# RWKV mixer: one schedule of rounds for heads, ends of heads and weight products, four buffer sets, joined products

## The chip, the cores and the metric

One core of a Trainium2 chip runs the whole kernel in one launch. The metric is the device time in microseconds (us) of one execution. 3 runs of the kernel before took 3470.03 to 3472.47 us, 3470.28 in the median.

## What is computed

Two transformer-like blocks, one after the other, on 256 tokens of width 2048, in float32. The first has a state-space mixer, latent attention and a convolutional feed-forward part. The second has the stage of this case: it normalises, multiplies by `w_in`, and gives parts of the product to an SSD mixer and to an RWKV-7 mixer with 32 heads of 64. The RWKV recurrence is

```
S = S * w_t + (S a_t) b_t^T + v_t k_t^T ;   y_t = S r_t
```

followed by a group norm of `y` per head, a bonus (the sum over `r * k * r_k`, times `v`) and a gate `g = sigmoid(gd) @ g2`. The change touches the order and the form of the work on RWKV, and which weight products run beside it. The result is the same function.

## The kernel before

Five instruction streams (TensorE, VectorE, ScalarE, GpSimd, SyncE) are written out by Python generators, one function of the same name in each engine's program. A `yield` ends a step; `mix` takes so many steps of each generator in turn, which makes a *round*, and `flight` runs several of a kind side by side. Since every engine's program walks the same generators in the same order, the order of the work is set there. Every engine takes its instructions in order, and semaphores (`wait_ge`, `then_inc`) hand over between engines.

**Weight products.** `linear` (L611 in TensorE's program) multiplies a weight matrix tile by tile. A *block* is 128 x 128 weights: three matmuls (L622, L623, L624: high part by high, high by low and low by high part). SyncE loads weights, ScalarE rounds the high part of a piece of up to 1024 columns (8 blocks; `cut_to`, L1889), VectorE subtracts to get the low part (L1073). In this stage a tile has 16 blocks (2 in `L_g2`) and its result is in one of two PSUM banks; VectorE scales it (`raw_shift`, L1466), ScalarE and VectorE make the token shift (L2097, L1476). `step` says how many blocks go into one step: 4 in `L_krv`, 8 in `L_sm` and `L_x`.

**A pair of heads.** `i` is a tile of 128 channels, which is two heads of 64; the code calls the work on it `pair(i)`. `krv` fills `KK(i)`, `AR(i)`, `VV(i)` for two `i` at a time (`b` is that group; below "a pair" is the two `i` of one `b`). `prep(i)` computes decay and keys (VectorE L1540 to L1581, with a reciprocal at L1568). `solve(b)` makes a triangular system in PSUM (L828), which VectorE turns (L1606, L1610) and GpSimd solves in 62 small operations (L2475, L2479); VectorE turns it back in `finish` (L1589). `block(i, hf)` works on 128 tokens, in 12 steps on TensorE: four transposes (L843 to L846), two steps of products that VectorE masks (L855, L856; L1632), `az` (L862; copied at L1636), the products with the inverse (L869, L870; its diagonal blocks are written by L1641, the result copied at L1647), `q` and the first part of the output `y0` (L876 to L882; `y0` is copied by ScalarE, L2171), `g` (L887), four chunks of 32 tokens (L897 to L901, state copied by VectorE L1663 for one half and ScalarE L2177 for the other), and a last one, where VectorE adds the chunks' outputs to `y0` (L1668). L1625 and L1627 make `bx` and `kx`, keys split by chunk. After two blocks `pair` has the tail: group norm, bonus (L911 to L919; VectorE L1684 to L1703, with a reciprocal at L1694). The next `pair` with the same parity starts only when the tail's last operation (L1703) is done.

**The order around it.** After `L_sm` and `L_krv[0]`, for b = 0 to 8, one `mix` runs `pair(2b-2)`, the weights `main(b)`, `pair(2b-1)`, and `prep` and `solve` of b. Both heads go in step. At b = 7 and 8 the weights are those of the SSD mixer (`L_bc`, `L_x`). Three buffer sets `BUF` hold k, r, v, b of three pairs. `turn_dt` (L1743) begins the next stage.

## Time and profile before

| | us |
|---|---|
| median of 3 runs | 3470.28 |
| the profiled execution, its own time | 3470.51 |
| its span, first to last instruction | 3468.4 |
| TensorE busy | 3073.7 |
| VectorE busy | 2319.8 |
| ScalarE busy | 1460.5 |
| GpSimd busy | 649.9 |

In the rows below PE is TensorE's matmul, PEld its weight load, DVE VectorE, ACT ScalarE, POOL GpSimd. `m` is an SBUF tile, `bank` a PSUM tile. Matmuls overlap in the pipeline, so TensorE's pace is read from the start of one to the start of the next. A float32 matmul appears as two instructions.

### The profile page before, as it was taken

What the parts mean: (1) busy time and instruction counts of PE and PEld (TensorE: products, weight loads), DVE (VectorE), ACT (ScalarE), POOL (GpSimd) and SP (SyncE); (2) the same over time, 40 slices, a digit from 0 to 9 for tenths busy, and PEclk for the clock granted to TensorE, in tenths of its full rate; (3) what the DMA queues carried; (4) which work ended last, traced back from release to release, by engine and by line L of the source; (5) the groups of instructions that cost most, each with busy time, mean ns of one, the idle gap of its engine ahead of it and who ended that gap; (6) DMA issues with size and microseconds to landing.
All of it is one profiled execution on the core that took longest, in us unless ns stands there. A gap on an engine that the chain in (4) does not pass through costs nothing.

```text
span 3468.4 us, 49760 instructions
## 1 busy us (share of the span) xinstructions
PE 3073.7 (89%) x19562; PEld 2716.6 (78%) x19562; DVE 2319.8 (67%) x4024; ACT 1460.5 (42%) x2307; POOL 649.9 (19%) x827
## 2 busy tenths in 40 slices
PE   5756799999999997788888888988899999999998
PEld 5645578888888887677777777986788888888887
DVE  8787467775587657677777776766575666556655
ACT  3222355554455544332333333345444444344443
POOL 5332001210021100444433334000010011001100
PEclk9877799999999998899999989999899999999999
DMA  4211145555555555212111212342355555555554
GB/s 186 89 49 49 62 150 177 188 185 176 194 193 189 167 178 176 90 63 77 68 60 65 75 68 83 119 152 76 107 170 177 178 192 183 176 200 188 189 169 147
DMA packets 78806, 475.16 MB, mean 137 GB/s; under 512 B 8112, under 2 KB 11184, under 8 KB 37424
## 3 DMA queue, kind: packets, MB, share of 16 engines
q1 hardware_dynamic: 76480, 459.66, 38.9%
q10 hardware_dynamic: 2096, 12.32, 1.0%
q8 instruction: 158, 2.59, 0.3%
q14 instruction: 72, 0.59, 0.0%
HBM read 465.66 MB, written 6.29 MB: 136 GB/s over the span
## 4 chain that ended last, share of the span: by engine, by line
PE 73%; DVE 19%; ACT 4%; issue 2%; POOL 1%; DMA 0%; DVEq 0%; SPq 0%; ACTq 0%
PE bank L620 32%; PE bank L624 20%; PE bank L622 4%; PE bank L623 4%; DVE m L1073 3%; PE bank L636 2%; ACT m L1889 1%; PE bank L899 1%; DVE m L1330 1%; DVE m L1694 1%; DVE m L1568 1%; DVE m L1723 1%; PE bank L901 1%; PE bank L900 1%; POOL m L2475 1%
## 5 line engine op out<-in xcount | busy, mean ns | idle before, releaser
L624 PE MATMUL bank<-m,m 128*128 128x256 f32 x6864 | 1951.0, 284 | 0.0
L620 PE MATMUL bank<-m,m 128*128 128x512 f32 x4992 | 1759.4, 396 | 32.0 <-DVE m L1173 13.0
L1073 DVE TENSOR_TENSOR m<-m,m 128x1024 fp32r<-128x1024 f32 (+2 forms) x944 | 1068.8, 1139 | 651.6 <-ACT m L1889 638.3
L624 PEld LDWEIGHTS bank<-m,m 128*128 128x128 f32 x6864 | 1321.8, 193 | 1.5
L1889 ACT ACTIVATE m<-m 128x1024 fp32r<-128x1024 f32 (+2 forms) x944 | 914.3, 980 | 829.1 <-PE bank L624 812.6
L620 PEld LDWEIGHTS bank<-m,m 128*128 128x128 f32 x4992 | 942.4, 189 | 248.0 <-DVE m L1173 14.9
L622 PE MATMUL bank<-m,m 128*128 128x256 f32 x1872 | 586.3, 313 | 78.4 <-DVE m L1073 45.9
L623 PE MATMUL bank<-m,m 128*128 128x256 f32 x1872 | 550.4, 294 | 0.0
L622 PEld LDWEIGHTS bank<-m,m 128*128 128x128 f32 x1872 | 380.4, 203 | 112.3 <-issue 68.5
L623 PEld LDWEIGHTS bank<-m,m 128*128 128x128 f32 x1872 | 380.7, 203 | 4.5 <-issue 3.8
L2456 POOL TENSOR_TENSOR m<-m,m 128x256 fp32r<-128x256 f32 x44 | 63.3, 1439 | 703.3 <-ACT m L2081 703.3
L2479 POOL TENSOR_TENSOR m<-m,m 128x31 f32<-128x31 f32 (+15 forms) x248 | 162.8, 657 | 19.4
L2475 POOL TENSOR_TENSOR m<-m,m 128x31 f32<-128x31 f32 (+15 forms) x248 | 153.6, 619 | 19.5
L2447 POOL TENSOR_TENSOR m<-m 128x256 f32<-128x256 f32 x44 | 32.7, 742 | 453.9 <-DVE m L1438 453.9
L2177 ACT ACTIVATE m<-bank,m 64x64 f32<-64x64 f32 x128 | 38.9, 308 | 159.3 <-PE bank L901 158.8
L636 PE MATMUL bank<-m,m 128*128 128x256 f32 x268 | 76.0, 401 | 13.0 <-ACT m L1911 12.2
L2450 POOL TENSOR_TENSOR m<-m,m 128x256 fp32r<-128x256 f32 x44 | 63.3, 1439 | 123.3 <-ACT m L2058 123.3
L2468 POOL MEMSET m<- 128x1024 f32 x8 | 7.6, 952 | 418.3 <-DVE m L1610 418.3
L2064 ACT ACTIVATE m<-bank 128x256 f32<-128x256 f32 x88 | 34.0, 386 | 116.2 <-PE bank L624 116.2
L2518 POOL TENSOR_TENSOR m<-m,m 128x256 fp32r<-128x256 f32 x8 | 6.9, 894 | 368.7 <-ACT m L2321 368.7
L2097 ACT ACTIVATE m<-m,m 128x256 f32<-128x256 f32 (+1 forms) x52 | 26.4, 507 | 116.1 <-DVE m L1466 116.0
L1443 DVE TENSOR_TENSOR m<-m,bank 128x256 f32<-128x256 f32 x88 | 37.0, 421 | 56.7 <-ACT m L2064 56.7
(361 smaller groups left out, 3268.5 us busy)
## 6 DMA issues: line engine op xcount, KB each, us to landing
m<-in_w_up SPq DMA_DIRECT2D x88, 1024.0 KB, 4.8
m<-in_w_down SPq DMA_DIRECT2D x128, 704.0 KB, 4.0
m<-in_w_gu SPq DMA_DIRECT2D x88, 1024.0 KB, 4.9
m<-in_w_out SPq DMA_DIRECT2D x48, 1024.0 KB, 5.0
m<-in_w_krv SPq DMA_DIRECT2D x48, 1024.0 KB, 4.9
m<-in_w_xbc SPq DMA_DIRECT2D x24, 1024.0 KB, 4.9
m<-in_w_z SPq DMA_DIRECT2D x16, 1024.0 KB, 4.9
m<-in_w_in SPq DMA_DIRECT2D x14, 1024.0 KB, 4.9
```

The lines of the kernel that those rows point to most:

```text
L620: pe.matmul(both, hi, x, start=kc == L.k0, stop=False)
L622: pe.matmul(ps, hi, x[:, 0, :], start=kc == L.k0, stop=False)
L623: pe.matmul(ps, hi, x[:, 1, :], start=False, stop=False)
L624: m = pe.matmul(ps, lo, x[:, 0, :], start=False, stop=last)
L636: pe.matmul(banks[N.bank][:, 0:T], ones, square_of(N, i), start=i == 0, stop=i == N.nk - 1).then_inc(*norm_pe(("sq", q)))
L1073: v.tensor_tensor(lo_of(k), raw_of(k)[0], hi_of(k).bitcast(F32), SUB).then_inc(*lo_v(("lo", k)))
L1889: a.activation(hi_of(k), src, ACT.Copy).then_inc(*hi_a(("hi", k)))
L2177: a.activation(sn[R, R], bB[R, R], ACT.Copy, scale=PL[R, i, hf * 4 + c:hf * 4 + c + 1]).then_inc(*wkv_a(("s", i, hf, c)))
L2450: g.tensor_tensor(far[:, 1, j % 22, :], s[:, 1, :], far[:, 0, j % 22, :].bitcast(F32), SUB).then_inc(*ffn_g(("lo", j)))
L2456: g.tensor_tensor(far[:, 1, j % 22, :], cvs2[j % 4], far[:, 0, j % 22, :].bitcast(F32), SUB).then_inc(*ffn_g(("lo2", j)))
L2475: g.tensor_tensor(prod, XB[:, r + 1:32, r:r + 1].broadcast_to([128, n, r + 1]), XX[:, r:r + 1, 0:r + 1].broadcast_to([128, n, r + 1]), MUL ...
L2479: g.tensor_tensor(x5, x5, prod, ADD).then_inc(*wkv_g(*([("x", b)] if r == 30 else [])))
```

## The change

`second_mixer` gives one schedule for all engines. A round has one step of an even head, two steps of weights, one of an odd head, three of weights, one of the ends of heads (`tail`), one of `prep`/`solve` (`after`). All weight products of the stage have `step=1`, one block a step. `prep` of pair b begins in round 27 + 20 b, its heads in round 56 + 20 b, odd heads five rounds later; a head takes 20 rounds, `block` has ten steps. `tail(i)` runs beside the next pair, in banks 2 and 3 and with buffers of its own. There are four buffer sets, so weights of two pairs ahead can be made. `L_g2[0]` comes after `L_krv[3]`, and so on; `L_x` is cut in 6 and 10 tiles with `L_g2[6]` and `L_g2[7]` behind them. In a block: ScalarE copies all four transposes, `az` and `wu` (VectorE did two of them); `bx` is made from the SBUF copy, `kx` is replaced by a product over 32 rows; both masks are one VectorE operation, both diagonal blocks another; the two products with the inverse are one; the chunks' outputs accumulate in PSUM on `y0`; what a head's first chunk multiplies by the zero state is left out.

```diff
+def timed(*items):
+    n = 0
+    for begin, g in items:
+        while n < begin:
+            n += 1
+            yield
+        for _ in g:
+            n += 1
+            yield
+AFTER, PAIRS, ROUNDS = 27, 56, 20
+def second_mixer(main, block, tail, after, *early):
+    def heads(e):
+        return timed(*((PAIRS + ROUNDS * b + 5 * e, chain(block(2 * b + e, 0), block(2 * b + e, 1))) for b in range(8)))
+    tails = timed(*((PAIRS + ROUNDS * (i // 2 + 1) + 5 * (i % 2), tail(i)) for i in range(16)))
+    afters = timed(*((AFTER + ROUNDS * b, after(b)) for b in range(8)))
+    run(mix((heads(0), 1), (main, 2), (heads(1), 1), (main, 3), (tails, 1), (afters, 1), *((g, 1) for g in early)))
...
-        BUF = [(alloc(2, 2, 2, 128), alloc(2, T), alloc(2, T), alloc(2, T)) for _ in range(3)]
+        BUF = [(alloc(2, 2, 2, 128), alloc(2, T), alloc(2, T), alloc(2, T)) for _ in range(4)]
...
+            return BUF[(i // 2 + 2) % 4][0][:, i % 2]
...
-        L_sm = linear("w_sm", 4, 16, TWO, lambda t: wkv_v["raw", t])
-        L_krv = [linear("w_krv", 6, 16, TWO, lambda t: wkv_v["raw", 4 + t], step=4)]
...
+        L_sm = linear("w_sm", 4, 16, TWO, lambda t: wkv_v["raw", t], step=1)
+        L_krv, L_g2, L_x = [], [], []
+        def g2(b):
+            L_g2.append(linear("w_g2", 2, 2, TWO, lambda t: wkv_v["gate", t], t0=2 * b, step=1))
+        for b_ in range(8):
+            if b_ >= 4:
+                g2(b_ - 4)
+            L_krv.append(linear("w_krv", 6, 16, TWO, lambda t: wkv_v["raw", 4 + t], t0=6 * b_, step=1))
+        g2(4)
+        L_bc = linear("w_xbc", 8, 16, TWO, lambda t: ssd_v["raw", t], t0=16, step=1)
+        g2(5)
+        for t0, nt in ((0, 6), (6, 10)):
+            L_x.append(linear("w_xbc", nt, 16, TWO, lambda t: ssd_v["raw", t], t0=t0, step=1))
+            g2(6 + len(L_x) - 1)
...
-                if hf:
-                    pe.wait_ge(*wkv_v["y2", i, 0])
-                elif i >= 2:
-                    pe.wait_ge(*wkv_v["out", i - 2])
+                if before:
+                    pe.wait_ge(*wkv_a["y", *before])
...
-                for e in range(2):
-                    R, b = HALVES[e], (bB, bA)[e]
-                    if e:
-                        pe.wait_ge(*wkv_v["kx", i, hf])
-                    elif hf:
-                        pe.wait_ge(*wkv_v["s", i, 0, 3])
-                        pe.wait_ge(*wkv_a["s", i, 0, 3])
+                pe.wait_ge(*wkv_a["tk", i, hf])
+                if before:
+                    pe.wait_ge(*wkv_v["s", *before, 3])
+                    pe.wait_ge(*wkv_a["s", *before, 3])
+                for e, R, b in ((0, HALVES[0], bA), (1, HALVES[1], bB)):
                     pe.matmul(b[:, 0:128], BB(i)[R, TS], AR(i)[R, hf, 1, :], start=True, stop=True)
+                for e, R, b in ((0, HALVES[0], bA), (1, HALVES[1], bB)):
                     pe.matmul(b[:, 128:384], KK(i)[R, TS], AR(i)[R, hf, :, :].rearrange("p a b -> p (a b)"),
                               start=True, stop=True).then_inc(*wkv_pe(("mk", i, hf, e)))
-                    yield
-                pe.wait_ge(*wkv_a["tk", i, hf])
-                pe.wait_ge(*wkv_v["mk", i, hf, 1])
+                yield
+                pe.wait_ge(*wkv_v["mk", i, hf])
...
-                    xb = xbd[2 * e_ + e]
-                    pe.matmul(bA[:, 64 * e:64 * e + 64], xb, tk[:, 0, 64 * e:64 * e + 64], start=True, stop=True)
-                    m = pe.matmul(bA[:, 128 + 64 * e:192 + 64 * e], xb, az[e_][:, 64 * e:64 * e + 64], start=True,
-                                  stop=True)
+                    m = pe.matmul(bA[:, 0:256].rearrange("p (a b) -> p a b", a=2)[:, :, 64 * e:64 * e + 64],
+                                  xbd[e_][:, e, :], tk[:, TZ:TV, 64 * e:64 * e + 64], start=True, stop=True)
...
                 pe.wait_ge(*wkv_v["g", i, hf])
                 for c in range(4):
+                    Q, first = slice(32 * c, 32 * c + 32), hf == c == 0
+                    sb_ = sbd[2 * e_ + c % 2]
                     if c:
                         pe.wait_ge(*wkv_v["s", i, hf, c - 1])
                         pe.wait_ge(*wkv_a["s", i, hf, c - 1])
-                    sb_ = sbd[2 * e_ + c % 2]
-                    pe.matmul(bA[:, 32 * c:32 * c + 32], sb_, qb[:, 32 * c:32 * c + 32], start=True,
-                              stop=True).then_inc(*wkv_pe(("yc", i, hf, c)))
-                    pe.matmul(bB[:, 0:128], bxb[:, c, :], wub[:, 128:256], start=True, stop=False)
-                    pe.matmul(bB[:, 0:128], kxb[:, c, :], tk[:, 1, :], start=False, stop=False)
-                    pe.matmul(bB[:, 0:128], gb[:, c, :], sb_, start=False, stop=True).then_inc(
-                        *wkv_pe(("s", i, hf, c)))
-                    yield
-                yield
+                    if not first:
+                        m = pe.matmul(bA[:, Q], sb_, qb[:, Q], start=False, stop=c == 3)
+                        if c == 3:
+                            m.then_inc(*wkv_pe(("y", i, hf)))
+                    pe.matmul(bB[:, 0:128], bxb[:, c, :], wub[:, 0:128], start=True, stop=False)
+                    m = pe.matmul(bB[:, 0:128], tk[Q, TK, :], tk[Q, TV, :], start=False, stop=first)
+                    if not first:
+                        m = pe.matmul(bB[:, 0:128], gb[:, c, :], sb_, start=False, stop=True)
+                    m.then_inc(*wkv_pe(("s", i, hf, c)))
+                    yield
...
+            def tail(i):
                 e = i % 2
+                b, b2 = banks[2 + e], banks[3 - e]
+                pe.wait_ge(*wkv_a["y", i, 1])
+                if i:
+                    pe.wait_ge(*wkv_v["out", i - 1])
+                for k in range(2):
+                    pe.wait_ge(*wkv_v["xa", min(i // 2 + 2, 7), k])
+                pe.matmul(b[:, 0:T], blk, ybs[e], start=True, stop=True).then_inc(*wkv_pe(("t1", i)))
                 yield
                 pe.wait_ge(*wkv_a["t2", i])
+                pe.matmul(b2[:, 0:T], blk, tails[1], start=True, stop=True).then_inc(*wkv_pe(("t2", i)))
                 pe.wait_ge(*wkv_v["t3", i])
+                pe.matmul(b[:, 0:T], blk, ybs[e], start=True, stop=True).then_inc(*wkv_pe(("t3", i)))
+                yield
...
-                v.tensor_tensor(bxb, bA[:, 256:384].unsqueeze(1).broadcast_to([128, 4, 128]), m4, MUL).then_inc(
-                    *wkv_v())
-                v.tensor_tensor(kxb, bA[:, 384:512].unsqueeze(1).broadcast_to([128, 4, 128]), m4, MUL).then_inc(
-                    *wkv_v(("kx", i, hf)))
+                else:
+                    v.wait_ge(*wkv_g["zero"])
                 yield
                 for e in range(2):
                     v.wait_ge(*wkv_pe["mk", i, hf, e])
-                    v.tensor_tensor(mk[e].rearrange("p a b -> p (a b)"), (bB, bA)[e][:, 0:384], m3, MUL).then_inc(
-                        *wkv_v(("mk", i, hf, e)))
-                    yield
-                v.wait_ge(*wkv_pe["az", i, hf])
-                v.tensor_copy(az[e_], bB[:, 0:128]).then_inc(*wkv_v())
+                v.tensor_tensor(mk.rearrange("p e a b -> p e (a b)"),
+                                pair_.rearrange("p (e x) -> p e x", e=2)[:, :, 0:384],
+                                m3.unsqueeze(1).broadcast_to([128, 2, 384]), MUL).then_inc(*wkv_v(("mk", i, hf)))
+                yield
                 finish(i // 2)
                 v.wait_ge(*wkv_v["xt", i // 2])
-                for e in range(2):
-                    ln = hf * 4 + i % 2 * 2 + e
-                    v.tensor_tensor(xbd[2 * e_ + e].rearrange("p (c t) -> p c t", c=4),
-                                    XTs[i // 2 % 2][:, :, ln].unsqueeze(1).broadcast_to([128, 4, 32]),
-                                    bm.rearrange("p (c t) -> p c t", c=4), MUL).then_inc(
-                        *wkv_v(*([("xb", i, hf)] if e else [])))
-                yield
-                v.wait_ge(*wkv_pe["wu", i, hf])
-                v.tensor_copy(wub, bA[:, 0:256]).then_inc(*wkv_v(("wu", i, hf)))
+                ln = hf * 4 + i % 2 * 2
+                v.tensor_tensor(xbd[e_].rearrange("p e (c t) -> p e c t", c=4),
+                                XTs[i // 2 % 2][:, :, ln:ln + 2].rearrange("p t e -> p e t").unsqueeze(2).broadcast_to(
+                                    [128, 2, 4, 32]),
+                                bm.rearrange("p (c t) -> p c t", c=4).unsqueeze(1).broadcast_to([128, 2, 4, 32]),
+                                MUL).then_inc(*wkv_v(("xb", i, hf)))
+                yield
+                v.wait_ge(*wkv_a["tk", i, hf])
+                v.tensor_tensor(bxb, tk[:, TB, :].unsqueeze(1).broadcast_to([128, 4, 128]), m4, MUL).then_inc(
+                    *wkv_v(("bx", i, hf)))
                 yield
...
-                v.tensor_tensor(ybuf[:, TS], ybuf[:, TS], bA[:, 0:128], ADD).then_inc(*wkv_v(("y2", i, hf)))
...
-                a.activation(tokb[e_].rearrange("p a b -> p (a b)"), bA[:, 0:256], ACT.Copy).then_inc(
-                    *wkv_a(("tk", i, hf)))
-                for _ in range(5):
-                    yield
-                a.wait_ge(*wkv_pe["y0", i, hf])
-                if hf == 0 and i >= 2:
-                    a.wait_ge(*wkv_v["out", i - 2])
-                a.activation(ybs[e_][:, TS], bA[:, 0:128], ACT.Copy).then_inc(*wkv_a(("y0", i, hf)))
+                if hf or i >= 2:
+                    a.wait_ge(*wkv_pe["s", *((i, 0) if hf else (i - 2, 1)), 3])
+                a.activation(tk[:, TA:, :].rearrange("p a b -> p (a b)"), bA, ACT.Copy).then_inc(*wkv_a(("tk", i, hf)))
+                yield
+                yield
+                a.wait_ge(*wkv_pe["az", i, hf])
+                a.activation(tk[:, TZ, :], bB[:, 0:128], ACT.Copy).then_inc(*wkv_a(("az", i, hf)))
+                yield
+                a.wait_ge(*wkv_pe["wu", i, hf])
+                a.activation(wu[e_], bA[:, 0:256], ACT.Copy).then_inc(*wkv_a(("wu", i, hf)))
+                yield
                 yield
                 yield
                 for c in range(4):
                     R, sn = HALVES[1], sbd[2 * e_ + (c + 1) % 2]
+                    if c == 3:
+                        a.wait_ge(*wkv_pe["y", i, hf])
+                        if i >= 2:
+                            a.wait_ge(*wkv_v["out", i - 2])
+                        a.activation(ybs[e_][:, TS], bA[:, 0:128], ACT.Copy).then_inc(*wkv_a(("y", i, hf)))
...
```

## Rows read from the trace of the kernel before

**Rows 1.** The page: busy time and share of the span by engine.

```profile
PE 3073.7 (89%) x19562; PEld 2716.6 (78%) x19562; DVE 2319.8 (67%) x4024; ACT 1460.5 (42%) x2307; POOL 649.9 (19%) x827
```

**Rows 2.** Windows of the stage: us, busy (instructions) of five engines, clock, DMA, GB/s.

```profile
1310.00:1357.00 47.00, 30.63 (x221) 29.67 (x221) 39.05 (x69) 18.17 (x25) 4.32 (x9) 0.82 0.24 81
1357.00:1387.00 30.00, 29.30 (x250) 29.13 (x249) 17.53 (x23) 14.20 (x18) 0.00 (x0) 1.00 0.93 329
1387.00:1434.40 47.40, 38.05 (x307) 36.99 (x306) 35.47 (x61) 21.82 (x31) 15.43 (x21) 0.93 0.35 116
1434.40:1533.50 99.10, 78.71 (x574) 70.36 (x573) 62.97 (x128) 29.37 (x56) 64.61 (x104) 0.86 0.19 65
1672.00:1770.50 98.50, 83.47 (x623) 74.85 (x621) 71.55 (x151) 33.02 (x62) 40.54 (x64) 0.93 0.20 70
```

**Rows 3.** The line at which the next stage begins: ns, first and last start.

```profile
L1743 DVE COPY m<-bank x1: 224/224/224, 2317.1 to 2317.1; 128x64 f32<-128x64 f32 x1
```

**Rows 4.** TensorE's waits in one period, 1672 to 1770.5: us, times, longest.

```profile
PE bank L843 <- DVE m L1703: 5.6, 1, 5.6
PE bank L869 <- DVE m L1641: 2.7, 2, 2.3
PE bank L828 <- DVE m L1581: 2.1, 1, 2.1
...
PE bank L897 <- DVE m L1663: 1.2, 1, 1.2
```

**Rows 5.** Timeline of TensorE, full clock: start us, us, what, instructions in a row.

```profile
1623.10 0.39 PE L900 MATMUL bank<-m,m 128*128 128x128 f32 x2
...
1623.32 0.39 PE L901 MATMUL bank<-m,m 128*128 128x128 f32 x2
...
1712.38 0.39 PE L870 MATMUL bank<-m,m 128*128 128x64 f32 x2
1712.60 0.39 PE L869 MATMUL bank<-m,m 128*128 128x64 f32 x2
...
1714.00 0.38 PE L622 MATMUL bank<-m,m 128*128 128x256 f32 x1
1714.22 0.28 PE L623 MATMUL bank<-m,m 128*128 128x256 f32 x1
1714.34 0.28 PE L624 MATMUL bank<-m,m 128*128 128x256 f32 x1
```

**Rows 6.** VectorE's groups in that period: busy us, mean ns, idle before them.

```profile
L1073 DVE TENSOR_TENSOR m<-m,m 128x1024 fp32r<-128x1024 f32 (+1 forms) x13 | 15.9, 1221 | 4.9 <-ACT m L1889 4.9
L1632 DVE TENSOR_TENSOR m<-bank,m 128x384 f32<-128x384 f32 x8 | 4.3, 548 | 0.8 <-PE bank L856 0.8
...
L1476 DVE SCALAR_TENSOR_TENSOR m<-m,m,m 128x256 f32<-128x256 f32 x6 | 3.6, 608 | 3.5 <-ACT m L2097 3.5
L1568 DVE RECIPROCAL m<-m 128x256 f32<-128x256 f32 x2 | 3.5, 1753 | 0.1
...
L1641 DVE TENSOR_TENSOR m<-m,m 128x128 f32<-128x128 f32 x8 | 3.3, 447 | 0.0
L1627 DVE TENSOR_TENSOR m<-bank,m 128x512 f32<-128x512 f32 x4 | 2.7, 678 | 0.0
...
L1647 DVE COPY m<-bank 128x256 f32<-128x256 f32 x4 | 1.7, 422 | 3.0 <-PE bank L870 3.0
...
L1636 DVE COPY m<-bank 128x128 f32<-128x128 f32 x4 | 1.1, 280 | 0.0
...
L1668 DVE TENSOR_TENSOR m<-m,bank 128x128 f32<-128x128 f32 x4 | 0.9, 270 | 0.0
```

**Rows 7.** L1641 with `solve` running, then without; GpSimd's L2479 from the page.

```profile
L1641 DVE TENSOR_TENSOR m<-m,m x4: 369/485/717, 1609.3 to 1611.0; 128x128 f32<-128x128 f32 x4
...
L1641 DVE TENSOR_TENSOR m<-m,m x4: 373/379/381, 1664.8 to 1665.9; 128x128 f32<-128x128 f32 x4
...
L2479 POOL TENSOR_TENSOR m<-m,m 128x31 f32<-128x31 f32 (+15 forms) x248 | 162.8, 657 | 19.4
```

More of the change, by code:

```diff
@@ L942, in turn_dt, with after @@
+            def after(b):
+                yield from flight(lambda i: prep(2 * b + i), 2, 2)
+                yield from solve(b)
             def turn_dt():
@@ L1029, in tensor_program @@
                            *(L_up[q].freed(44 * q + t) for t in range(40, 44)), done=sums_ if q else None))
[L1030 to L1039 removed]
+            second_mixer(main(), block, tail, after, iter(range(8)), last_squares(sums_))
             turn_dt()
@@ L1493, in steps_dt @@
                 a, e, w, p = (q[R, :] for q in scr[0:4])
-                yield
+                for _ in range(5):
+                    yield
                 v.wait_ge(*wkv_v["dt"])
@@ L1840, in vector_program @@
             v.wait_ge(*wkv_v.last)
-            run(mix((chain(linear(L_sm, small), linear(L_krv[0], krv)), 1), (steps_dt(), 1),
-                    (both_rates(ffn_v.last), 1)))
-            v.wait_ge(*wkv_g["zero"])
-            for b in range(9):
-                before = [pair(2 * b - 2 + i) if b > 0 else iter(()) for i in range(2)]
-                after = chain(flight(lambda i: prep(2 * b + i), 2, 2), solve(b)) if b < 8 else iter(())
-                run(mix((before[0], 1), (main(b), 1), (before[1], 1), (after, 1)))
-            run(linear(L_g2[7], gated))
-            v.wait_ge(st_y[7 % 3], 16 * (7 // 3 + 1))
+            second_mixer(main(), block, tail, after, steps_dt(), both_rates(ffn_v.last))
+            for b in (5, 6, 7):
+                v.wait_ge(st_y[b % 3], 16 * (b // 3 + 1))
             turn_dt()
@@ L2116, in steps_dt @@
                 R = slice(96, 128)
-                yield
+                for _ in range(5):
+                    yield
                 a.wait_ge(*dt_v["w"])
@@ L2153, in prep @@
                 yield
-                yield
             def solve(b):
@@ L2179, in block, with tail @@
                     yield
-                yield
-            def pair(i):
-                s1, s2 = tails[2 * (i % 2)], tails[2 * (i % 2) + 1]
-                for hf in range(2):
-                    yield from block(i, hf)
+            def tail(i):
+                s1, s2 = tails
                 a.wait_ge(*wkv_v["t1", i])
@@ L2301, in both_rates @@
                 a.dma_start(a2s[0:96, :], d["a2"]).then_inc(ld_a2, 16)
-            run(mix((chain(linear(L_sm, small), linear(L_krv[0], krv)), 1), (steps_dt(), 1), (both_rates(), 1)))
-            a.wait_ge(*wkv_g["zero"])
-            for b in range(9):
-                before = [pair(2 * b - 2 + i) if b > 0 else iter(()) for i in range(2)]
-                after = chain(flight(lambda i: prep(2 * b + i), 2, 2), solve(b)) if b < 8 else iter(())
-                run(mix((before[0], 1), (main(b), 1), (before[1], 1), (after, 1)))
-            run(linear(L_g2[7], lambda t: None))
-            store(7)
+            second_mixer(main(), block, tail, after, steps_dt(), both_rates())
             for b in (5, 6, 7):
@@ L2506, in pool_program @@
                 run(linear(L_down[q]))
-            run(linear(L_sm, small))
-            g.wait_ge(*norm_v["lo", N_two.x0 + 15])
-            for q in (XA, *gt, *sbd):
-                g.memset(q, 0.0).then_inc(*wkv_g(*([("zero",)] if q is sbd[-1] else [])))
-            for b in range(9):
-                before = [pair() if b > 0 else iter(()) for i in range(2)]
-                after = chain(flight(lambda i: iter(range(5)), 2, 2), solve(b)) if b < 8 else iter(())
-                run(mix((before[0], 1), (main(b), 1), (before[1], 1), (after, 1)))
+            second_mixer(main(), block, tail, after)
             g.wait_ge(ld_y, 16)
```

249 lines of the change are left out of this document (126 added, 123 removed).

## The prediction

> **What bounds the kernel now.** I read the page first for the span and the shares: TensorE is busy 89% of it and VectorE 67% [rows 1], so TensorE is the engine to watch, but a mean over the span says nothing of the stage that is changed. So next the windows, cut at the stage's own marks [rows 2]: from 1310 us, where the first `L_sm` matmuls start, to 2317.1, where `turn_dt` copies [rows 3], is 1007 us. It has three parts: 77 us with weights alone, 47 us with the first `prep`, and then periods of 98.5 to 99 us, each of which does 100 blocks of weights and one pair (two tiles `i`). In such a period (1672 to 1770.5) TensorE is busy 83.5 us of 98.5, VectorE 71.6, ScalarE 33.0 [rows 2]. So 15.0 us per period are idle on TensorE, and its granted clock is 0.93: about 14% of the time at 1.2 and the rest at 2.4 GHz. The work in those 14% (13.8 us) would take half as long at the full clock, so the clock costs up to 6.9 us, and the period's work at 2.4 GHz is 83.5 - 6.9 = 76.6 us. No engine is the bound: 22 us of each 98.5 are waits and what they cost in clock. The waits of TensorE say which [rows 4]: 5.6 us for the last operation of a head's tail (L1703 to L843), 2.7 for the diagonal blocks of the inverse (L1641), 2.1 for `prep` (L1581), the rest smaller.
>
> **What a change can get at most.** The stage has 1248 blocks (64 of `L_sm`, 768 of `L_krv`, 32 of `L_g2`, 384 of `w_xbc`). A block is three matmuls of 0.12 us start to start at the full clock (1714.22 to 1714.34 [rows 5]), 0.36 us, so 449 us. A pair's own work is 76.6 - 36 = 40.6, eight of them 325. Together 774, against 1007: 233 us are there to be had.
>
> **The change, step by step.** One round now has five blocks of weights, and a pair has 20 rounds. I count the 250 rounds (1248 / 5) in four stretches.
>
> Rounds 0 to 27 (135 blocks). Before, the first 80 blocks took 47 us (to 1357), with VectorE busy 39 of them and the clock at 0.82; the next 83 took 30 [rows 2]. The rates and the `steps_dt` chain are the same instructions, four rounds later, with less to do per round but five blocks instead of eight to hide them. I take the same 47, and 55 blocks at 0.36: 67 us.
>
> Rounds 27 to 56 (145 blocks, two `prep` and `solve`, no heads). The window with one of each and 96 blocks took 47.4 [rows 2], 13 over its weights. A round's cover is five blocks instead of four, so I take 10 over the weights for each: 145 x 0.36 + 20 = 72 us.
>
> Rounds 56 to 216 (eight pairs, 800 blocks), x us each, less 7 for the two pairs with no `prep` beside them (38.05 busy less 34.6 of weights [rows 2] is 3.5 for one). Now x.
> - TensorE. The joined `wu` product halves its instructions: 8 of the 16 pairs of L869 and L870 go. A pair is 0.22 us start to start with 64 columns, and with 128 too (L900 to L901) [rows 5], so -1.8. More turns between weights and heads, each 0.1 over the usual step (1714.00 to 1714.22 against 1714.22 to 1714.34 [rows 5]), perhaps ten more: +1. The K = 32 product instead of `kx` streams the same columns: 0. Two products less in a head's first chunk: under 0.1. 76.6 - 1.8 + 1 = 75.8.
> - VectorE. `kx` (2.7), the copies of `az` (1.1) and `wu` (1.7), the sum of the outputs (0.9) and a memset (0.3, too small to list) go [rows 6]. Two masks in one: 384 columns take 0.548, and L1627 shows 512 in 0.678, 1.02 ns per column, so 768 take 0.94 instead of 1.10: -0.6 for four. The diagonal blocks in one: between 0.57 (the slope again) and 0.88 (no gain) instead of 0.88, I take 0.7: -0.7. `bx` now reads SBUF instead of PSUM: L1641, which reads SBUF twice, took 373 to 381 ns with GpSimd quiet and up to 717 with `solve` running [rows 7]; so 0 to 0.34 more, four times, +0.6 at the middle. Sum -7.4, so 64.2 busy. Waits inside its line that stay: 4.9 for the high part of a cut and 3.5 for the shift's first half [rows 6]. 73 us of work and fixed waits per period, under TensorE's 76.
> - On that port: the Trainium skill, SBUF — State Buffer (the section on what causes contention), says that a VectorE operation with two SBUF inputs and a GpSimd operation that reads SBUF take one shared port pair as an exclusive lock, and the loser waits. By that rule a whole GpSimd operation, 0.66 us on the mean (L2479 [rows 7]), could stand before each `bx`: 2.6 us instead of 0.6, VectorE at 75, still under TensorE, and the sum the same. The trace agrees in kind.
> - ScalarE takes the two copies (0.28 and 0.42 each on VectorE, L1636 and L1647 [rows 6]; I take the same) and a `tk` of twice the width (256 columns more, 0.3): 4 x 1.0, so 37 of some 85 busy. Cover: 48 us idle. Its copies stand in line behind a 1 us cut, so the price is a late copy at worst.
> - The stall of 5.6 us at the next head's first transposes goes: they wait now for the copy of the previous output (`y`), and the tail has four rounds of its own; the next to wait for it is `gate`, four rounds later. What is late next: VectorE in `prep`. A `prep` and `solve` of a pair is 35.5 - 96 x 0.21 = 15.3 us of VectorE (0.21 a block by the window before it [rows 2]), now in eight rounds: 1.9 each, on the 2.4 of the rest (49 / 20), 4.3 against TensorE's 3.8, and two of them hold two reciprocals of 1.75 each [rows 6]. Eight such rounds leave it 4 us or more behind, and its slack is less than a round: 3 us idle. Every other handoff (mask to `az`, `q` to `g`, `g` to chunk, sums to the next chunk) has at least two or three blocks and the other head's step between: 0 if VectorE is on time, up to the old 9.4 (15.0 - 5.6) if not; I take 3.5. So 6.5 idle.
> - Clock: 6.9 went with 15 idle; with 6.5, 2.7 by proportion. Bounds 0 and 6.9.
> x = 75.8 + 6.5 + 2.7 = 85. Eight times, less 7: 673 us.
>
> Rounds 216 to 250 (168 blocks, last tail, two gates, the wait for the last store): 60.5 + 4.5 = 65 us.
>
> Priced at nothing: the fourth buffer set and the index shift (no work moves); the loads' order on SyncE (same bytes, at 70 GB/s [rows 2]); GpSimd's memsets placed inside the stream (it idles for them); ScalarE's wait for the saved `h` (eight rounds, 14 us, lie between; if not landed it holds cuts for a few us, once).
>
> Sum: 67 + 72 + 673 + 65 = 877, against 1007: -130. The profiled execution took 3470.5 us with a span of 3468.4, the median of the runs is 3470.3, so the execution and the median are the same for this purpose. 3470 - 130 = **3340 us**. A change within 0.2% (7 us) is what a measurement here can't tell from none.
>
> **Rivals.**
> 1. The waits stay, elsewhere. VectorE (73) and TensorE (76) are so near each other that two lines kept in step by in-order waits lose as much as before. For it: VectorE already shows 27 us of waits per period, and the row of cuts among them. Against: its load falls by 8. x = 95: 130 - 80 = 50 gained, 3420. The Trainium skill has a rule that ends in the same place (TensorE: Matmul & The Clock Gate, section on the second HAM failure mode: short idles between groups of matmuls in every iteration let the clock go back and forth). As rows: at 0.86, as in 1434 to 1533 [rows 2], 75.8 us of work take 88, and with 6.5 idle x is again 95. Against it, the period with 15 us idle still has 0.93 [rows 2].
> 2. TensorE nearly fed: 1 us idle, no clock lost, x = 78: 56 more, 3284.
> 3. Slower: each of 20 rounds ends on one handoff that isn't covered. The place is the sum of a chunk: VectorE's copy of it for the even head stands behind the cut, the shift and the tail operations of the round before, and the next chunk's matmul waits. It decides from x = 101.3, that is 16.3 us or 0.8 per round over my x. A cut (1.22) ahead of the copy in every round would do it: 20 x 1.22 = 24 us, x = 109, 3532. Against: now TensorE waits 1.2 us in a period for these copies (L897 behind L1663 [rows 4]), and only 13 cuts come in 20 rounds [rows 6].
> 4. It doesn't do what it says: the period is held by a chain that the change keeps (GpSimd's `solve`, 40.5 busy of 98.5 [rows 2]). The diagonal blocks now wait for it 24 rounds after its start, so there is no such hold. It gives 3470.
>
> **Chances.** Forecast (3300 to 3385) 0.58; first rival 0.22; second 0.14; third 0.03; fourth 0.03. The range reaches from the second rival's end to the first's: 3285 to 3420. Faster 0.94, same 0.02, slower 0.04.
>
> **What the profile after would show.** Period between the first reciprocals of `prep` near 85 us instead of 98.5; TensorE's idle time before the first transposes gone; VectorE busy near 64 per period; ScalarE near 37; clock over 0.95 between the pairs; the last tail some 30 rounds before the stage's end. I am wrong if TensorE's waits for VectorE's sums or masks sum to over 10 us per period, if the clock falls below 0.9, or if the stretch before the first head grows past 150 us.

## The result, and the profile after

The changed kernel takes 3479.24 us (median of 11 runs, 3477.6 to 3481.77), the kernel before 3471.84 beside it (11 runs): ratio 1.0022, 95% interval 1.0013 to 1.0031. It is slower by 7 us, little but clear of the interval, where 130 us less were forecast. The profiled execution took 3480.06 us.

The stage ends where `turn_dt` copies, as in [rows 3]:

```profile
L1771 DVE COPY m<-bank x1: 225/225/225, 2328.0 to 2328.0; 128x64 f32<-128x64 f32 x1
```

Counted from the same mark, 1310 us, the stage takes 1018 us where it took 1007. The mark is round: the last product of the stage ahead of it starts at 1300.5 us before, at 1303.3 in the changed kernel, 1303.8 in e7 and 1300.6 in e9 (runs below), so 3 us of a first stretch can be its arrival. The page's busy line, beside [rows 1]:

```profile
PE 3109.5 (89%) x19370; PEld 2725.0 (78%) x19370; DVE 2276.2 (65%) x3816; ACT 1496.4 (43%) x2375; POOL 666.1 (19%) x827
```

VectorE has the 44 us less work, ScalarE the 36 us more. TensorE has 192 matmuls less and is busy 36 us longer. Windows of the stage (columns as in [rows 2]): up to the first head's transposes in two parts, two periods, the stretch after the last pair has begun, the whole stage:

```profile
1310.00:1393.00 83.00, 60.34 (x449) 58.78 (x448) 52.64 (x87) 31.24 (x42) 3.87 (x9) 0.85 0.47 159
1393.00:1483.70 90.70, 63.27 (x439) 60.62 (x440) 64.31 (x103) 35.10 (x52) 46.23 (x64) 0.83 0.27 93
1667.40:1762.50 95.10, 88.39 (x598) 76.23 (x597) 65.70 (x125) 36.89 (x70) 42.75 (x65) 0.89 0.21 73
1762.50:1855.30 92.80, 84.73 (x598) 72.87 (x597) 65.75 (x125) 36.89 (x70) 42.24 (x65) 0.94 0.22 75
2139.10:2328.00 188.90, 163.23 (x1134) 146.91 (x1133) 110.98 (x190) 76.61 (x122) 0.00 (x0) 0.89 0.29 100
1310.00:2328.00 1018.00, 885.00 (x6117) 782.35 (x6117) 670.25 (x1203) 398.85 (x692) 345.98 (x521) 0.90 0.25 87
```

The kernel before over its whole stage:

```profile
1310.00:2317.10 1007.10, 842.87 (x6294) 767.98 (x6294) 714.39 (x1410) 363.01 (x624) 329.59 (x521) 0.92 0.25 87
```

TensorE's idle time did fall, from 164 us to 133; its busy time rose by 42, in fewer matmuls at a lower clock. VectorE's waits in the whole stage, of the kernel before and then of the changed one (us, times, longest):

```profile
DVE m L1073 <- ACT m L1889: 78.6, 79, 2.7
DVE m L1663 <- PE bank L901: 40.9, 37, 3.5
```

```profile
DVE m L1107 <- ACT m L1911: 154.2, 129, 3.6
DVE m L1510 <- ACT m L2119: 31.7, 52, 0.9
```

L1107 (L1073 before) is VectorE's half of a cut, the low part; it needs the high part that ScalarE makes (L1911, L1889 before). That wait has doubled, and it is the largest in the stage. TensorE's own list is short and mixed (25.1 us of the first row and 15.6 of the second lie ahead of the first head):

```profile
PE bank L652 <- DVE m L1500: 40.8, 9, 17.2
PE bank L861 <- DVE m L1616: 25.9, 8, 8.0
PE bank L899 <- DVE m L1670: 10.9, 9, 3.3
PE bank L849 <- ACT m L2166: 10.9, 6, 2.9
```

How the wait comes about stands in the timelines of TensorE, ScalarE and VectorE (start us, us, what, and in brackets the idle time before):

```profile
1688.94 0.27 PE L878 MATMUL bank<-m,m 128*128 128x128 f32 x1
...
1689.26 0.60 ACT L2189 ACTIVATE m<-bank 128x512 f32<-128x512 f32 x1 [2.77 <-PE bank L878]
1689.88 1.06 ACT L1911 ACTIVATE m<-m 128x1024 fp32r<-128x1024 f32 x1
...
1690.97 1.23 DVE L1107 TENSOR_TENSOR m<-m,m 128x1024 fp32r<-128x1024 f32 x1 [1.98 <-ACT m L1911]
1692.23 0.42 DVE L1703 SCALAR_TENSOR_TENSOR m<-bank,m 128x256 f32<-128x256 f32 x1
1692.69 0.49 DVE L1706 SCALAR_TENSOR_TENSOR m<-m,m,m 128x256 f32<-128x256 f32 x1
1693.09 0.27 DVE L1694 TENSOR_SCALAR m<-bank,m 64x64 f32<-64x64 f32 x1
1693.29 0.94 DVE L1663 TENSOR_TENSOR m<-bank,m 128x768 f32<-128x768 f32 x1
```

ScalarE's cut waits for nothing itself. It stands behind the copy of four transposes (L2189), for which ScalarE has waited 2.77 us. (This copy is of two transposes in the kernel before; `az` and `wu` are the two that are new on ScalarE.) VectorE reaches its own half of the same piece in the same step, so it waits for ScalarE's queue, and behind it stand the tail's first operations, a chunk's sums (L1694) and a mask (L1663).

By stretches (a table put together from the start times of a pair's first transposes; us; "later" is VectorE's half of a cut one piece later, the runs below):

```
                                  to 1st head   7 periods   rest    stage
before                                  124.5       725.0   157.6  1007.1
predicted                               139         591.5   146.5   877
after                                   173.7       655.4   188.8  1018.0
e1  masked keys back                    172.0       641.4   181.1   994.5
e9  later                               157.6       613.8   165.1   936.5
e7  masked keys back, later             161.0       596.8   162.7   920.5
e10 the same, later in all linears      152.5       596.8   162.7   912.0
```

### The profile page after: what moved, and what is told of

Its sections match the earlier page's. It is cut to its first block, busy times and chain, and to the rows that moved or that the text cites. A ratio compares the mean times of both kernels' runs of the same rounds, so it can differ in the third digit from the quotient of the medians.

```text
span 3478.0 us, 49231 instructions
## 1 busy us (share of the span) xinstructions
PE 3109.5 (89%) x19370; PEld 2725.0 (78%) x19370; DVE 2276.2 (65%) x3816; ACT 1496.4 (43%) x2375; POOL 666.1 (19%) x827
## 4 chain that ended last, share of the span: by engine, by line
PE 75%; DVE 17%; ACT 5%; issue 2%; DMA 1%; DVEq 0%; ACTq 0%; POOL 0%; SPq 0%
PE bank L650 32%; PE bank L654 20%; PE bank L652 5%; PE bank L653 4%; DVE m L1107 3%; ACT m L1911 2%; PE bank L666 2%; PE bank L931 1%; DVE m L1744 1%; PE bank L933 1%; DVE m L1364 1%; PE bank L930 1%; DVE m L1603 1%; PE bank L916 1%; PE bank L899 1%
## 5 line engine op out<-in xcount | busy, mean ns | idle before, releaser
L654 PE MATMUL bank<-m,m 128*128 128x256 f32 x6864 | 1958.4, 285 | 0.0
L1107 DVE TENSOR_TENSOR m<-m,m 128x1024 fp32r<-128x1024 f32 (+1 forms) x944 | 1071.3, 1142 | 730.6 <-ACT m L1911 717.0
L1911 ACT ACTIVATE m<-m 128x1024 fp32r<-128x1024 f32 (+1 forms) x944 | 913.8, 979 | 826.1 <-PE bank L654 806.1
L652 PE MATMUL bank<-m,m 128*128 128x256 f32 x1872 | 610.0, 326 | 104.7 <-DVE m L1107 44.8
L653 PE MATMUL bank<-m,m 128*128 128x256 f32 x1872 | 555.8, 297 | 0.0
L2512 POOL TENSOR_TENSOR m<-m,m 128x31 f32<-128x31 f32 (+15 forms) x248 | 175.5, 707 | 19.4
L2508 POOL TENSOR_TENSOR m<-m,m 128x31 f32<-128x31 f32 (+15 forms) x248 | 157.8, 636 | 19.5
L666 PE MATMUL bank<-m,m 128*128 128x256 f32 x268 | 77.2, 407 | 13.0 <-ACT m L1933 12.2
```

What stands on the lines that cost most here:

```text
L652: pe.matmul(ps, hi, x[:, 0, :], start=kc == L.k0, stop=False)
L653: pe.matmul(ps, hi, x[:, 1, :], start=False, stop=False)
L654: m = pe.matmul(ps, lo, x[:, 0, :], start=False, stop=last)
L666: pe.matmul(banks[N.bank][:, 0:T], ones, square_of(N, i), start=i == 0, stop=i == N.nk - 1).then_inc(*norm_pe(("sq", q)))
L1107: v.tensor_tensor(lo_of(k), raw_of(k)[0], hi_of(k).bitcast(F32), SUB).then_inc(*lo_v(("lo", k)))
L1911: a.activation(hi_of(k), src, ACT.Copy).then_inc(*hi_a(("hi", k)))
```

## The experiments

The runs are called by the first part of their names, e1 for `e1_kx`. All times are medians beside the kernel before, which gave 3471 to 3473 us each time.

**The two terms suspected first.** The changed kernel with the masked keys of before, and the kernel before without them:

```diff
-m = pe.matmul(bB[:, 0:128], tk[Q, TK, :], tk[Q, TV, :], start=False, stop=first)
+m = pe.matmul(bB[:, 0:128], kxb[:, c, :], tk[:, TV, :], start=False, stop=first)
```

> The changed kernel with one thing undone: the product of a chunk that takes 32 token rows out of 128 is again a product of all 128 rows with a masked copy of the keys (two masked copies of 128x512 a head on VectorE in place of one). Theory 1, the 32-row product costs TensorE a change of its row window: a chunk goes back from 1.19 us to 0.89 us from first product to next linear piece; 16 chunks a period of two heads, so 4.8 us a period less TensorE time, eight periods: 38 us, so about 3441 us for 3479. Theory 2, VectorE bounds the period (65.7 us busy and waits for cuts): TensorE's gain turns into waits and VectorE's extra 2 x 1.3 us or so a period lengthen it: 3479 to 3500 us.

> The kernel before with one thing done: the masked copy of the keys goes, and the chunk's key-value product takes 32 of the 128 token rows. Theory 1 (the 32-row product costs 0.3 us a chunk on TensorE): 128 chunks, of which the period's TensorE is the bound, so +38 us at most, less what the 1.3 us copy per head gives back where its wait was on the path: 3490 to 3510 us for 3471. Theory 2 (the product costs nothing by itself, the changed kernel loses in its schedule): 3471 or up to 15 us less.

e1 took 3459.28 us, 20 less than the changed kernel, and e2 3515.88, 44 more than the kernel before. So the 32-row product, which I had priced at nothing, costs; e2 is 6 us past theory 1's range. A chunk in the changed kernel, then in e1:

```profile
1703.12 0.30 PE L927 MATMUL bank<-m,m 128*128 128x32 f32 x2
1703.26 0.47 PE L930 MATMUL bank<-m,m 128*128 128x128 f32 x2
1703.65 0.48 PE L931 MATMUL bank<-m 32*128 32x128 f32 x2
1704.07 0.49 PE L933 MATMUL bank<-m,m 128*128 128x128 f32 x2
1704.31 0.37 PE L652 MATMUL bank<-m,m 128*128 128x256 f32 x1
```

```profile
1691.61 0.30 PE L927 MATMUL bank<-m,m 128*128 128x32 f32 x2
1691.75 0.47 PE L930 MATMUL bank<-m,m 128*128 128x128 f32 x2
1692.05 0.39 PE L931 MATMUL bank<-m,m 128*128 128x128 f32 x2
1692.28 0.39 PE L933 MATMUL bank<-m,m 128*128 128x128 f32 x2
1692.42 0.37 PE L652 MATMUL bank<-m,m 128*128 128x256 f32 x1
```

From L927 to the next weights it is 1.19 us with the 32-row product and 0.81 without, 0.38 a chunk. The chunks with four products and the full clock have the same medians in the two traces (95 of them in the changed kernel, 99 in e1). 128 chunks are 49 us. In the kernel before the price shows nearly in full, though the edit also takes a masked copy off VectorE and widens one on ScalarE. In the changed one less than half of it comes back:

```profile
1659.60:1751.90 92.30, 79.56 (x598) 70.72 (x597) 67.99 (x129) 36.92 (x70) 43.70 (x64) 0.93 0.22 75
```

TensorE is busy 5 to 9 us less in e1's period, and idle 12.7 us instead of 6.7 and 8.1. Something else holds the period. Theory 1 had the mechanism and twice its worth; theory 2 is against the sign, but its thought that VectorE holds the period was not refuted.

**The start as before.** Its edit, in short: `L_sm` in steps of eight and `L_krv[0]` in steps of four run ahead of the rounds, and `AFTER, PAIRS` are 0 and 29.

> The changed kernel with the start of the mixer as before: the small linear in steps of eight and the first key-receptance-value block in steps of four run beside the rate work before the rounds begin, and the rounds carry blocks 1 to 7. Theory 1 (the start's one-by-one steps lose the time, 55.5 us for the first 80 pieces where VectorE normalises 16 tiles in the way): the first head's transposes come 15 to 20 us earlier than 1483.7 us, the rest as it was, about 3462 us. Theory 2 (the start only moves a wait that the rounds after it take back): within 5 us of 3479.

3523.15 us, 44 slower; the first transposes came 3 us earlier, not 15 (the "pieces" of the expectation are blocks of 128 rows). Both theories fall. The experiment changed more than it meant to: the linears now stand five rounds otherwise against the heads, and with that the period from 1674.7 us is 102.2 us long. Why this phase is so bad stays open.

**Both halves of the cut later.** For VectorE and for ScalarE:

```diff
 if what == "piece":
-    cut_to(at_ + CUT)
+    cut_to(at_ + CUT - (1 if L.step == 1 else 0))
```

> The changed kernel with VectorE and ScalarE cutting each evacuated piece one step later in their order (a piece of lead less), linears in steps of one only. Theory 1 (VectorE and TensorE go in lockstep: VectorE waits 12.7 us a period for cuts that it asks for a piece too early): these waits fall to about 4 us, the period by 2 to 5 us, total 15 to 35 us less: about 3455 us. Theory 2 (the waits are slack of an engine that does not bound): no change, 3474 to 3484 us.

3470.26 us, 9 less, between the two theories. Its waits for cuts in the period from 1658.4 us did not fall, against theory 1:

```profile
DVE m L1107 <- ACT m L1911: 12.8, 11, 3.9
DVE m L1510 <- ACT m L2119: 3.9, 6, 0.9
```

With both halves moved VectorE still asks in the step in which ScalarE makes its half. So the ring of four buffers, which TensorE must free, isn't what VectorE waits for. The two edits together:

> The masked keys of the run e1_kx (3459.3 us) together with the later cuts of e4_lead (3470.3 us for 3479.2 of the changed kernel). Theory 1, the two costs are separate (TensorE's row window in the period, and the pieces' ring in the stretches before and after the heads): they add, 3450 us. Theory 2, both come out of the same wait (VectorE's handoffs): no more than one of them counts, 3458 to 3460 us.

3458.77 us: theory 2's number; the 9 us did not add.

**VectorE's half alone one piece later.** The same line in VectorE's program only, ScalarE as it was:

> The masked keys of e1_kx, and the later cut on VectorE alone: ScalarE still cuts at once, VectorE one piece later, so that VectorE finds its half ready. Theory 1 (VectorE's 12.7 us a period of waits for ScalarE's half of the cut delay its handoffs to TensorE): these waits fall below 4 us a period, TensorE's waits for masks and sums (some 9 us a period in e1_kx) fall by 2 to 4 us, total 3425 to 3445 us. Theory 2 (VectorE has that slack anyway): 3455 to 3462 us, as e1_kx.

3382.27 us (ratio to before 0.9743, 0.9728 to 0.9758), 77 less than e1, more than theory 1 gave. On the changed kernel without another edit, and on the kernel before (there for steps of four):

> The changed kernel with the one edit that brought e7_kx_vlead from 3459.3 to 3382.3 us: VectorE makes its half of a piece's cut one piece later than ScalarE. Theory 1 (the chain piece read by TensorE, ScalarE's half, VectorE's half, which VectorE waits for in front of everything else it has to do, is what the one-by-one steps brought; it costs the whole 77 us by itself): 3479 less 60 to 80 us, 3400 to 3420 us, and beside e7 the 32-row product then costs 20 to 40 us. Theory 2 (with the 32-row product TensorE's own work bounds the period, so that half the gain is covered): 3430 to 3450 us.

> The kernel before with VectorE's half of a cut one piece later in the linears with steps of four. Theory 1 (the wait came with the change, by its one-by-one steps; before, VectorE waits 4.9 us a period for ScalarE's half): 0 to 25 us less than 3471. Theory 2 (the wait costs both kernels the same, and the change lost elsewhere): 60 to 80 us less, 3390 to 3410 us.

e9 took 3398.18 us, 81 less than the changed kernel; e11 3447.39, 25 less than the kernel before beside it. Both are theory 1's numbers (e9 2 us past its range), but beside e7 the 32-row product costs 16 us and not the 20 to 40 expected. The later request is worth more than three times as much in the changed kernel, where it also takes more wait away: 154.2 to 4.1 us in the stage, for 78.6 to 29.7 in e11, which leaves the linears with other steps as they were.

The comparison that leaves least beside the wait is e9 with e4. VectorE's program is the same in both, with the same order of cuts, masks and sums. Only ScalarE's half stands a piece later in e4, and e4 takes 72 us more. So the gain isn't that VectorE's own cut of 1.2 us gave way to other work; it is that ScalarE's half is ready when VectorE asks for it. e9's whole stage, one of its periods, its last stretch, and the two largest waits of VectorE in the stage:

```profile
1310.00:2246.50 936.50, 842.59 (x6124) 745.44 (x6123) 668.58 (x1202) 399.13 (x692) 357.71 (x521) 0.95 0.28 95
...
1640.20:1729.00 88.80, 82.41 (x599) 70.96 (x598) 65.49 (x125) 36.93 (x70) 44.57 (x64) 0.96 0.23 78
...
2081.40:2246.50 165.10, 153.18 (x1152) 138.88 (x1150) 110.40 (x190) 76.70 (x122) 0.00 (x0) 0.98 0.35 117
```

```profile
DVE m L1694 <- PE bank L933: 49.9, 37, 3.5
DVE m L1500 <- PE bank L654: 44.7, 24, 3.8
```

The work is the same: as many matmuls but for a few that a trace misses, and on VectorE and ScalarE the same busy time within 2 us. VectorE's waits are now for TensorE: it is ahead of it, where it was behind. TensorE is idle 94 us instead of 133, which is 39 of the 81.5, and busy 42 less in the same matmuls at a clock of 0.95 instead of 0.90. In a middle period nearly all of it is the second: 95.1 us with 6.7 idle became 88.8 with 6.4. These are the stretches of the two periods by granted clock, first the changed kernel's, then e9's:

```profile
1667.40:1724.50 57.10, 54.03 (x396) 46.76 (x394) 37.71 (x69) 21.82 (x44) 41.00 (x62) 1.00 0.23 79
1724.50:1731.30 6.80, 5.98 (x27) 4.82 (x28) 4.39 (x11) 4.96 (x10) 0.00 (x0) 0.50 0.00 0
1731.30:1745.00 13.70, 12.38 (x86) 10.13 (x84) 9.24 (x16) 6.04 (x10) 0.00 (x0) 1.00 0.29 97
1745.00:1758.70 13.70, 12.19 (x59) 11.26 (x60) 11.20 (x27) 2.44 (x6) 0.00 (x0) 0.50 0.22 78
```

```profile
1640.20:1698.00 57.80, 54.24 (x396) 46.88 (x394) 38.95 (x69) 21.52 (x42) 44.57 (x64) 1.00 0.24 78
1698.00:1704.80 6.80, 5.41 (x24) 4.25 (x25) 5.05 (x13) 5.29 (x10) 0.00 (x0) 0.50 0.32 96
1704.80:1729.00 24.20, 22.77 (x180) 19.84 (x180) 21.49 (x44) 10.12 (x18) 0.00 (x0) 1.00 0.20 72
```

Both have 6.8 us at the lower of the clock's two levels (0.50, which is 1.2 GHz). The changed kernel has 13.7 us more of it from 1745.0 on, after TensorE had waited 0.3 us and 0.8 us for VectorE's and ScalarE's results; e9 has neither these waits nor the fall; its one wait from 1704.8 on, 1.4 us for `prep`, brought none. Over the seven periods the clock stood at the lower level for 116 us in the changed kernel and for 55 in e9.

The same place in a head in e9, VectorE's timeline:

```profile
1661.98 0.88 DVE L1687 TENSOR_TENSOR m<-bank,m 64x256 f32<-64x256 f32 x2 [0.88 <-PE bank L916]
1662.88 1.22 DVE L1107 TENSOR_TENSOR m<-m,m 128x1024 fp32r<-128x1024 f32 x1
1664.63 0.42 DVE L1703 SCALAR_TENSOR_TENSOR m<-bank,m 128x256 f32<-128x256 f32 x1 [0.52 <-PE bank L945]
...
1667.12 0.96 DVE L1663 TENSOR_TENSOR m<-bank,m 128x768 f32<-128x768 f32 x1 [1.27 <-PE bank L887]
```

The mask (L1663), which had stood in a row behind the late cut, is now waited for by VectorE until TensorE's product is there.

**What made the wait longer.** The changed kernel with the copies of `az` and `wu` on VectorE again (L2193 and L2196 off ScalarE):

> The changed kernel with the copies of the products az and wu on VectorE again, as before, and off ScalarE; nothing else. It tells why VectorE waits 12.7 us a period for ScalarE's half of a cut, 4.9 before. Theory 1 (the cut stands in ScalarE's line behind the two copies, which wait for TensorE): the waits fall to 5 to 8 us a period; VectorE takes 2.8 us more work, so that the period gains 1 to 5 us, 3440 to 3475 us. Theory 2 (the waits come from where the one-by-one steps put the cut among the steps of heads, whatever ScalarE carries): the waits stay over 11 us, and the period grows by the copies, 3485 to 3510 us.

3488.67 us, 9 more. VectorE's waits for cuts in the period that starts at 1670.4 us fell from 12.7 to 7.6, as theory 1 says; the time is theory 2's, 3485 to 3510, and not theory 1's, since VectorE's own work grew:

```profile
DVE m L1107 <- ACT m L1915: 7.6, 7, 2.0
```

So with the copies moved back 5 of the 8 us go that the wait grew by; over the seven periods it is 38.2 us in the kernel before, 90.9 in the changed one and 60.7 in e18. Part of the 30 can be that VectorE, with more work, asks later; this isn't separated. The moved copies are worth 9 us where they are, and it was their company with the cut that cost. The rest has other items in it: where the waits of the seven periods are followed back in the trace, about 22 of the 90.9 us stand behind the copies of `az` and `wu`, 10 behind that of the transposes, and 18 behind two small operations of `prep` and of the tail (L2175, L2218), for which ScalarE itself waits for VectorE.

**In all linears.** `- 1` for every linear of VectorE's program: with the masked keys, for the kernel before, and for the changed kernel alone:

> e7_kx_vlead with VectorE's later cut in every linear of the kernel, not only in those with steps of one. Theory 1 (the wait hurts only where VectorE has other work that TensorE waits for, in the two mixers): within 8 us of 3382. Theory 2 (it costs wherever pieces are cut): 20 us less or more.

> The kernel before with VectorE's half of each cut one piece later in every linear. It is the other side of e10_kx_vlead_all (3363 us) and e16_vlead_all. Theory 1 (the wait outside the mixer's rounds costs both kernels the same 19 us, which e10 gained over e7): 3447 less 15 to 23 us, 3424 to 3432 us, and the change proper, with the cut's wait gone from both, is worth 50 us. Theory 2 (the 19 us of e10 came from its own schedule): 3440 to 3448 us.

> The changed kernel with VectorE's half one piece later in every linear, and nothing else. Theory 1 (the 32-row product costs what e9_vlead less e7_kx_vlead showed, 16 us): 3363 plus 12 to 20 us, 3375 to 3383 us. Theory 2 (with all cuts out of the way TensorE's work is bare, and the product costs its whole 4.8 us a period): 3395 to 3402 us.

They took 3363.21, 3442.04 and 3383.93 us; e16 is 1 us past theory 1's range. Theory 1 of e10 (no gain elsewhere) falls: of the 24 us between the two profiled spans (3383.5 and 3359.3), 8.5 lie ahead of the first head and the rest outside the stage (4.5 of the 8.5 are there on arrival: the stage before ends at 1303.8 us in e7 and 1299.3 in e10). e13 gains only 5 over e11, where theory 1 wanted 15 to 23: outside the stage it has 12 less (3440.5 less 992.8 against 3443.7 less 983.5), and 9 of them are given back within it. Set e16 against e13 and the change is worth 58 us, ratio 0.983, once neither kernel has this wait. e16 against e10 prices the product at 21 us.

**The odd heads' offset.** `5 * e` taken out of `heads`, in the changed kernel and in e7:

> The changed kernel with one thing undone: the odd head of a pair in the same rounds as the even one instead of five rounds behind; the ends of heads stay where they are. Theory 1 (the offset spreads heavy rounds so that the waits of the two heads don't fall together): without it both heads' products for masks, sums and turns meet in the same rounds, and the period grows by 3 to 8 us, total 25 to 65 us more, 3505 to 3545 us. Theory 2 (each round is bound by TensorE's own work, wherever a head's steps lie): within 8 us of 3479.

> e7_kx_vlead with the odd head in the rounds of the even one instead of five behind. Theory 1 (the offset spreads the load, and the cuts' chain hid that in e6_instep, which took 3478.6 us for 3479.2): now it costs, 3395 to 3430 us. Theory 2 (the rounds are bound by work, wherever a step lies): 3378 to 3387 us.

3478.61 us for 3479.24: nothing. With the wait gone 3389.75 for 3382.27: the offset is worth 7 us, between the two theories. The changed kernel paid for it and didn't get it.

**Linear steps spread in the round.** In e8 (beside e5) and e15 (beside e10) the last of a round's five linear steps moves behind the step of the ends of heads; in e17 the five stand as two, one, one and one:

> e5_kx_lead with the last of a round's five linear steps moved behind the step of the heads' ends, so that the products of heads stand in three places between linear steps and not two. Theory 1 (what is left idle is the time that a head's product waits for VectorE within a round, covered by the linear steps between): TensorE's waits fall by 1 to 2 us a period, 8 to 15 us in all beside e5_kx_lead. Theory 2 (the idle comes from VectorE's order, not from TensorE's): no difference to e5_kx_lead beyond 4 us.

> e10_kx_vlead_all with the fifth linear step of a round moved behind the step of the heads' ends, as in e8 beside e5, where it gave 6 us. Theory 1 (steps of TensorE wait for VectorE within a round): 3350 to 3358 us. Theory 2 (that gain came out of the cuts' chain, now gone): within 4 us of 3363.

> e10_kx_vlead_all with a round's five linear steps as two, one, one and one between the steps of even heads, odd heads, ends and rates. Theory 1: as e15 and a little more, 3345 to 3358 us. Theory 2: within 4 us of 3363. If it spreads VectorE's evacuations against the heads' steps badly, 5 to 15 us more.

3452.36 us (6 less than e5), 3356.04 (7 less than e10), 3354.50 (9 less). Small and steady: e15 and e17 are theory 1's numbers, e8 lies between the two theories. e17 is the fastest: ratio to before 0.9661 (0.9647 to 0.9675), 117 us less, 125 less than the changed kernel.

## Why the prediction was wrong

**The step that failed** is the sentence on VectorE that "waits inside its line that stay: 4.9 for the high part of a cut", with the one on ScalarE: "its copies stand in line behind a 1 us cut, so the price is a late copy at worst". It is the other way round: the cut stands behind copies that wait for TensorE (and behind operations that wait for VectorE), and its lateness is handed to VectorE, which asks for it in the same step, ahead of all it owes TensorE. The wait went from 4.9 to 12.7 us a period and from 79 to 154 in the stage, and undone it gives 81 us of the 139 that I missed by. By my own sum VectorE then has 65.7 us of work, 12.7 for cuts and 3.9 for shifts, 82 us a period, over the 76 of TensorE and not under it. I had the row of this wait in my hand and filed it as fixed. My first rival named the mechanism (two lines kept in step by in-order waits, "the row of cuts among them") and got 95 for the period; the seven take 655.4, 93.6 each. The slower rival, a chunk's sums uncovered in every round, is not what happened, though the kernel did come out slower: TensorE's waits for sums and masks are under 4 us in the period from 1667.4, so the first of my three signs of error stayed silent. The other two came: a long start, and a clock under 0.9 (0.89 in that period, 0.91 over the seven).

**The 32-row product** "streams the same columns: 0". It costs 0.38 us a chunk on TensorE, 16 to 21 us in the changed kernel and 44 in the one before. The Trainium skill (TensorE: Matmul & The Clock Gate, section "Why this matters for your kernels") says that a single matmul with 32 rows takes the time of one with 128; among products of 128 rows in one chain this case's trace does not bear that out, and the measurement decides. What TensorE waits for there (its weights, or the products around) the runs don't tell.

**The start.** I foresaw 139 us to the first head; it is 173.7, beyond the 150 that I had named as a sign. 16 us of the 35 are gone in e9 (157.6), by the cuts' wait and up to 3 us of arrival; e10 has 152.5. Of the 13 left, 10 are in the stretch of the two `prep`, for which I took "10 over the weights for each", 72 us: from 1380 us to the first head e10 takes 82.5. TensorE's largest waits there, in e10:

```profile
PE bank L861 <- DVE m L1616: 14.4, 2, 8.0
PE bank L849 <- ACT m L2168: 7.5, 4, 2.6
```

L861 is the product of `solve`, and L1616 the last operation of `prep` on VectorE. With no head beside it, five blocks a round don't cover `prep`; the term should have been 15 and not 10. The other 3 us lie in the first stretch, where TensorE waits for VectorE's evacuation (L1500, up to 7.7 us).

**The period, 85 us.** With both causes undone (e7) seven periods take 596.8, 85.3 each. That the sum comes out is in part luck, since its parts don't: over the seven periods of e7 TensorE is idle 66.5 us, 9.5 each where I had 6.5, and busy 75.8 each where I had 78.5 of work and clock together. (The period shown below is one of the longer ones, with 10.3 idle.) In the changed kernel VectorE's work was forecast at 64.2 and is 65.7; the joined mask at 0.94 us is 0.95; ScalarE's 37 is 36.9. The stall of 5.6 at the next head's transposes is gone, as said.

```profile
1723.80:1812.30 88.50, 78.23 (x598) 70.41 (x597) 70.12 (x131) 36.88 (x70) 44.36 (x64) 0.94 0.23 78
```

**The last stretch**, 146.5 forecast, 188.8 measured, 165.1 without the wait. VectorE has 111 us of work there in either; e9's edit and what follows from it is all that lies between 188.8 and 165.1.

**The clock.** I gave it 2.7 us a period by proportion to idle time. It was 0.89 to 0.94 in periods with 6.7 and 8.1 us idle, and 0.96 in e9's with 6.4. So it doesn't follow the idle sum. The rule that I set beside the first rival (the Trainium skill, TensorE: Matmul & The Clock Gate, "A second HAM failure mode: psum-queue depth-cycling": short idles between groups in every iteration let the clock go back and forth) agrees in kind with the trace: half of what e9 gained came as busy time, and the fall at 1745.0 us came after waits of 0.3 and 0.8 us. What such a pause has to be to bring a fall isn't shown.

The sum of the misses: 35 before the heads, 64 in the periods, 42 after, 141 of the stage; 81.5 by e9's edit, 16 the product by e9 less e7, the other 43 in stretches of 22, 5 and 16. The 22 have 3 us of e7's later arrival in them and are else as named above; what the 16 of the last stretch are stays open.

## What to carry to other kernels

When two engines make halves of one thing in order, the second should ask for its half a step later than the first makes it: a `- 1` here, worth 25 us in one schedule and 81 in another, and nothing for the wait where both halves moved. Work moved to an engine that looks half idle is not only its own time; look at what stands behind it in that engine's line, and who waits for that. And a wait that the profile lists at a few microseconds is a quantity that the change can move, not a constant of the sum.

## What the runs showed of the hardware

A product of 32 rows between products of 128 rows added 0.38 us to a chunk (1.19 for 0.81, the medians of 95 and 99 chunks at the full clock), though it streams the same columns. In the same matmuls, TensorE was busy 885 us at a clock of 0.90 and 843 at 0.95, after the taking away of a wait that isn't TensorE's own. Its clock stood at 1.2 GHz for 13.7 us of a period after waits of 0.3 and 0.8 us for other engines, and in e9 the same work without these waits kept 2.4 GHz.
